# A chunked state scan on one NeuronCore: where TensorE waits for a sum, where VectorE adds it, and which engines weight and normalise

## The reference

```
states  = einsum('bcqgn,bcqgr,bcqgrp->bcgrpn', bc, to_end * dtc, xc)      # weighted x, outer product with B
h      -> h * chunk_decay + states                                         # scan over chunks
decay   = where(lower, exp(acum_i - acum_j), 0)                            # exponents of pairs of tokens
cb      = einsum('bcign,bcjgn->bcijg', cc, bc)                             # scores C.B
y_diag  = einsum('bcijg,bcijgr,bcjgr,bcjgrp->bcigrp', cb, decay, dtc, xc)
y_off   = einsum('bcign,cbgrpn,bcigr->bcigrp', cc, h_prev, exp(acum))
y       = y_forward + y_backward + d * x
y       = y * silu(z);   y = y * rsqrt(mean over the group of y*y + eps) * gain
```

## Time and profile before

| | |
|---|---|
| median of 3 runs | 3049.53 us (3045.53 to 3053.0) |
| the profiled execution, whole | 3047.3 us |
| its span, first to last instruction | 3045.6 us |
| mean granted TensorE clock, share of full | 0.983 |
| busy, share of the span | TensorE 94%, VectorE 57%, ScalarE 47%, GpSimd 16% |
| states stage | from 215.5 to 255.8 us |
| outputs stage | from 255.8 to 357.3 us |

### The profile page before, as it was taken

One profiled execution on the slowest core, in us unless ns is written; L12 is line 12 of the kernel. 1 busy time (PEld: TensorE's weight loads), 2 busy tenths in 40 slices (PEclk: granted clock), 3 DMA queues, 4 the chain that ended last, 5 costly groups with the idle time before them and its releaser, 6 DMA issues. The chain is left out here.

```text
span 3045.6 us, 37978 instructions
## 1 busy us (share of the span) xinstructions
PE 2876.4 (94%) x15242; PEld 2347.3 (77%) x15242; DVE 1738.3 (57%) x1950; ACT 1421.9 (47%) x1904; POOL 474.0 (16%) x581
## 2 busy tenths in 40 slices
PE   8998899898999899999999899999999998899998
PEld 4877797786887487777777478788888896788887
DVE  4437546445645788888888364555544316455543
ACT  4346427346223477887887132543333325443332
POOL 0002114123101623222222100000000003000000
PEclk9999899999999999999999999999999999899999
DMA  5220201112753589999999551123332301223331
GB/s 210 56 65 1 85 7 56 28 56 93 225 180 111 202 321 366 363 365 371 375 385 366 217 199 66 56 85 97 111 98 83 105 25 56 77 87 97 97 103 48
DMA packets 278527, 456.11 MB, mean 150 GB/s; under 512 B 24881, under 2 KB 206897, under 8 KB 258257
## 3 DMA queue, kind: packets, MB, share of 16 engines
q1 hardware_dynamic: 251856, 398.90, 37.2%
q0 software_dynamic: 26496, 54.79, 5.0%
HBM read 451.23 MB, written 39.08 MB: 161 GB/s over the span
## 5 line engine op out<-in xcount | busy, mean ns | idle before, releaser
L277 DVE TENSOR_TENSOR weight_part<-weights,weight_part 128x2048 fp32r<-128x2048 f32 (+1 forms) x62 | 140.5, 2267 | 153.5 <-ACT weight_part L266 153.5
L1206 ACT ACTIVATE up_conv<-banks,tap_columns 128x512 f32<-128x512 f32 x88 | 68.7, 781 | 288.4 <-PE banks L324 288.4
L266 ACT ACTIVATE weight_part<-weights 128x2048 fp32r<-128x2048 f32 (+1 forms) x62 | 115.9, 1870 | 164.1 <-PE banks L319 157.8
L1250 DVE SCALAR_TENSOR_TENSOR up_conv<-banks,tap_columns,up_conv 128x511 f32<-128x511 f32 x88 | 65.9, 749 | 214.1 <-ACT up_conv L1206 214.1
L319 PE MATMUL banks<-hT_r,weight_part 128*128 128x512 f32 x448 | 175.6, 392 | 0.3 <-PEq L3951 0.3
L324 PE MATMUL banks<-hT_r,weight_part 128*128 128x512 f32 x448 | 175.0, 391 | 0.0
L794 POOL TENSOR_SCALAR branch_mean<-branch_mean 128x1 f32<-128x1 f32 x20 | 10.7, 537 | 1047.8 <-ACT up_conv L788 704.8
L277 DVE TENSOR_TENSOR weight_part_o<-weights,weight_part_o 128x2048 fp32r<-128x2048 f32 (+2 forms) x46 | 100.0, 2174 | 115.2 <-ACT weight_part_o L266 115.2
L319 PE MATMUL banks<-hT_r,weight_part_o 128*128 128x512 f32 x384 | 149.5, 389 | 0.0
L323 PE MATMUL banks<-h_low,weight_part 128*128 128x512 f32 x384 | 149.4, 389 | 0.0
L323 PE MATMUL banks<-h_low,weight_part_o 128*128 128x512 f32 x384 | 149.4, 389 | 0.0
(11 more groups left out here) (742 smaller groups left out, 8701.0 us busy)
## 6 DMA issues: line engine op xcount, KB each, us to landing
weights<-in_w_e_gate SPq DMA_DIRECT2D x44, 1024.0 KB, 15.7
weights<-in_w_e_up SPq DMA_DIRECT2D x44, 1024.0 KB, 18.3
hT<-in_w_e_down SPq DMA_DIRECT2D x44, 1024.0 KB, 18.5
weights<-in_w_up SPq DMA_DIRECT2D x88, 512.0 KB, 4.9
gate_up<-in_w_e_gate SPq DMA_DIRECT2D x22, 1024.0 KB, 15.8
gate_up<-in_w_e_up SPq DMA_DIRECT2D x22, 1024.0 KB, 18.3
down<-in_w_e_down SPq DMA_DIRECT2D x22, 1024.0 KB, 18.6
weights<-in_w_down SPq DMA_DIRECT2D x20, 1024.0 KB, 4.9
```

The source lines that it names most:

```text
L266: c.nc.scalar.activation(self.pair(n)[0][:, 0:z], self.raw[n % RAW_SLOTS][:, 0:z], ACT.Copy).then_inc(self.high_ready, 1)
L277: c.nc.vector.tensor_tensor(low[:, 0:z], self.raw[n % RAW_SLOTS][:, 0:z], high[:, 0:z].bitcast(F32), ALU.subtract).then_inc(self.low_ready, 1)
L1206: nc.scalar.activation(a[:, f % 2, v], c.ps[:, 2 * (f % 4) + v], ACT.Identity, scale=conv[:, 2, ch:ch + 1], bias=bias[:, ch:ch + 1]).then_ ...
L1250: nc.vector.scalar_tensor_tensor(a[:, f % 2, v, 1:], c.ps[:, 2 * (f % 4) + v, 0:SEQ - 1], conv[:, 1, ch:ch + 1], a[:, f % 2, v, 1:], ALU.m ...
```

## The change

In the states, every item is weighted by two engines: GpSimd takes the first ten heads (640 columns), ScalarE the other six. TensorE waits for both. ScalarE's other work moves to earlier items, and two instructions that make `own` (the left sides of the exponent matmuls) move from the start of the outputs into the states. Twelve matmuls on the identity are added at the end of the states, behind a wait for the last but one state. `own` now lies in the space of B_T that held the SiLU and skip buffers, and these get a tensor of their own.

In the outputs, TensorE's wait for `ready` moves from ahead of the masks to behind the exponents. VectorE's sum moves ahead of the decays and the mix of the next unit. The norm moves from VectorE to GpSimd, behind the reciprocal root.

The diff, cut to its changed lines and what they stand in:

```diff
@@ -24,6 +24,7 @@
 DT_Z, ST_Z = 16, 6
+POOL_HEADS = 10
@@ -2151,6 +2152,7 @@
             masks = c.rounded(tri)
+            own = c.rounded(bT)[:, :, 0:2 * P]
@@ -2275,26 +2277,31 @@
                 act.wait_ge(wt_ready, 2)
-                for i in range(1, len(plan), 2):
+                for i in range(len(plan)):
...
                     to, rows, weights = weighs(i)
-                    for hd in range(SSD_H):
+                    for hd in range(POOL_HEADS, SSD_H):
...
                     last.then_inc(weighted[1], 1)
-                    if i == 1:
+                    if i == 0:
...
                         nc.scalar.activation(building_r, c.ps[:, 7], ACT.Copy).then_inc(rounded, 1)
-                    if i == 5:
+                    if i == 3:
...
                             nc.scalar.activation(exponents[:, :, hd], terms, ACT.Identity, scale=column(MOVES + hd), bias=column(STAYS + hd))
-                act.wait_ge(z_half, 1)
-                act.wait_ge(weighted[0], 2)
-                silu(0)
-                silu(1)
-                c.split.high(c, act)
+                    if i == 4:
+                        for d in range(2):
+                            nc.scalar.activation(own[:, :, d * P:(d + 1) * P], terms, ACT.Identity, scale=column(OWN + d), bias=column(ONE + d))
+                    if i == 6:
+                        act.wait_ge(z_half, 1)
+                        act.wait_ge(weighted[0], 4)
+                        silu(0)
+                        silu(1)
+                    if i == 7:
+                        c.split.high(c, act)
@@ -2302,12 +2309,13 @@
                 pool.wait_ge(wt_ready, 2)
-                for i in range(0, len(plan), 2):
+                for i in range(len(plan)):
...
                     to, rows, weights = weighs(i)
-                    nc.gpsimd.tensor_tensor(to.rearrange("p (h q) -> p h q", q=SSD_P), rows.rearrange("p (h q) -> p h q", q=SSD_P),
-                                            weights.unsqueeze(2).to_broadcast([P, SSD_H, SSD_P]), ALU.mult).then_inc(weighted[0], 1)
+                    n = POOL_HEADS
+                    nc.gpsimd.tensor_tensor(heads4(to[:, 0:n * SSD_P]), heads4(rows[:, 0:n * SSD_P]), weights[:, 0:n].unsqueeze(2).to_broadcast([P, n, SSD_P]),
+                                            ALU.mult).then_inc(weighted[0], 1)
@@ -2325,7 +2333,8 @@
                                 last.then_inc(z_half, 1)
-                    pe.wait_ge(weighted[i % 2], i // 2 + 1)
+                    for made in weighted:
+                        pe.wait_ge(made, i + 1)
@@ -2333,6 +2342,8 @@
                 assert len(left) <= ST_Z * (len(plan) - 1)
+                pe.wait_ge(kept, len(plan) - 1)
+                warm(c, 0, 12)
@@ -2352,7 +2363,7 @@
                         nc.vector.tensor_tensor(new, new, psum, ALU.add).then_inc(kept, 1)
-                    if i == 2:
+                    if i == 1:
@@ -2360,13 +2371,11 @@
         E = c.sb(s, "decays_of_pairs", [P, 3, 2, HG, P])
-        own = c.sb(s, "exponent_weights", [P, 2, NT, P], F32R)
+        gates = c.sb(s, "silu_and_skip", [P, 4, GP])
...
         rs = c.sb(s, "z_rstd", [P, SSD_G * NT])
-        lent = [bT[:, i, 0:CTX] for i in range(SSD_G)]
-        sz, skip = lent[0:2], lent[2:4]
+        sz, skip = [gates[:, n] for n in (0, 1)], [gates[:, n] for n in (2, 3)]
         sq = c.sb(s, "squares", [P, GP])
-        built = c.sem("so_exponents_built")
@@ -2387,7 +2396,6 @@
         def _(pool):
-            pool.wait_ge(built, 1)
@@ -2403,6 +2411,8 @@
                 nc.gpsimd.tensor_tensor(rs[:, at], rs[:, at], c.half[:, 0:1], ALU.pow).then_inc(rooted, 1)
+                pool.wait_ge(rooted, j + 1)
+                nc.gpsimd.tensor_scalar(rows_of(j), rows_of(j), rs[:, at], None, ALU.mult)
@@ -2411,20 +2421,18 @@
                     block_rows = slice(32 * g, 32 * g + 32)
-                    if i >= 2:
-                        pe.wait_ge(ready, i - 1)
-                        if lates(i - 1):
-                            pe.wait_ge(silud, lates(i - 1))
+                    if i >= 2 and lates(i - 1):
+                        pe.wait_ge(silud, lates(i - 1))
...
                                          start=True, stop=False)
-                    if i == 0:
-                        pe.wait_ge(built, 1)
                     for d in range(2):
-                        last = nc.tensor.matmul(c.ps[:, b + 1 + d], own[block_rows, d, tile], exponents[block_rows, tile].rearrange("p h n -> p (h n)"),
+                        last = nc.tensor.matmul(c.ps[:, b + 1 + d], own[block_rows, tile, d * P:(d + 1) * P], exponents[block_rows, tile].rearrange("p h n -> p (h n)"),
...
                     last.then_inc(decayed, 1)
+                    if i >= 2:
+                        pe.wait_ge(ready, i - 1)
@@ -2456,10 +2464,6 @@
 
-            for d in range(2):
-                last = nc.scalar.activation(own[:, d], terms, ACT.Identity, scale=column(OWN + d), bias=column(ONE + d))
-            last.then_inc(built, 1)
-            act.wait_ge(built, 1)
@@ -2479,10 +2483,6 @@
             L = lambda ins: c.vlink(dve, ins)
-
-            def norm(j):
-                dve.wait_ge(rooted, j + 1)
-                nc.vector.tensor_scalar(rows_of(j), rows_of(j), rs[:, j:j + 1], None, ALU.mult)
@@ -2500,16 +2500,14 @@
                     L(nc.vector.tensor_tensor(off[:, 0:GP], off[:, 0:GP], skip[j % 2], ALU.add))
+                    dve.wait_ge(diag, j + 1)
+                    nc.vector.tensor_tensor(rows_of(j), off[:, 0:GP], c.ps[:, 4 * (j % 2), GP:2 * GP], ALU.add).then_inc(ready, 1)
...
                     nc.vector.tensor_tensor(E[:, i % 3, 0], E[:, i % 3, 0], c.ps[:, 4 * (i % 2), 0:P].unsqueeze(1).to_broadcast([P, HG, P]), ALU.mult).then_inc(mixed, 1)
-                if i >= 4:
-                    norm(i - 4)
                 if i:
-                    dve.wait_ge(diag, j + 1)
-                    nc.vector.tensor_tensor(rows_of(j), off[:, 0:GP], c.ps[:, 4 * (j % 2), GP:2 * GP], ALU.add).then_inc(ready, 1)
@@ -2520,8 +2518,6 @@
                     c.split.low(c, dve)
-            for j in range(U - 3, U):
-                norm(j)
 def exponent_rows():
```

## The result

The changed kernel takes 3028.84 us in the median of six runs (3022.22 to 3033.18); the kernel before, timed beside it, 3052.17. One of the six executions of the kernel before was a slow one, 3255.83 us; the ratio leaves it out, and the median without it is 3051.34. The ratio is 0.9917, with a 95% interval from 0.9899 to 0.9935; the quotient of the two medians, 3028.84 / 3051.34 = 0.9926, lies inside it. The forecast was 3028. The execution that was profiled here took 3033.18 us with a span of 3031.5. That is 14.1 us less than the span of before, while the median won 23.3 (22.5 without that one execution).

The account below looks back on a forecast made before the run. In the outputs TensorE was taken to wait for a sum standing in VectorE's line behind another unit's exponentials. Terms -2.8 - 2.1 - 18.0 + 1.5 = -21.4 us from 3049.5 gave 3028, range 3021 to 3040.

Parts of the forecast that it names:

- The steady part: Outputs: TensorE no longer waits, so seven pairs of units take 9.68 us each, 67.8 against 85.8: -18.0 us.
- The room at the mix: Outputs: VectorE ends the mix at 5.3 us, TensorE needs it at 5.8, so 0.5 us to spare.
- The slow spells: Outputs: TensorE at granted clock 0.50 behind holes, costing 6.4 us over seven pairs; expected to go with the holes.
- The start of the outputs: First late unit's z starts 6.1 us behind the start of the outputs, not 8.21: -2.1 us (-2.5 to -1.5).
- The end of the outputs: From last SiLU to transposes, now 4.29 us: later last sum, longer last norm, +1.5 us (+0.5 to +2.5).
- The states: Shared weighting lets the outputs start at 253.0 to 253.1 against 255.79: -2.8 us (-3.2 to -1.8).
- The norm on GpSimd: Outputs: the moved norm costs GpSimd 0.85 us, hidden, coming later than the decays; hole taken as 0.
- signs of being wrong: Holes ahead of L2438, decays over 0.69 or gates over 0.43 us, norm over 1.05, or 0.50 clock without a hole.
- (a): Rival: half the holes in the outputs stay, 1 us a pair; gain -12 us, 3037; chance 0.17.
- (c): Rival: the wait for the sum becomes a wait for the mix, only the ends gain; -3.4 us, 3046; chance 0.06.
- (b): Rival: the holes go but slow spells stay, the clock falling for another cause; -15 us, 3034; chance 0.10.
- (d): Rival: GpSimd and VectorE always exclude each other, 13.1 us a pair; slower by 2.5 us, 3052; chance 0.05.

Follow-up runs that it names:

- holes_filled: The kernel before with six waste matmuls put into each hole ahead of a late unit's masks: seven pairs 79.28 us against 85.83, whole ratio 0.9995.
- states_only: The changed kernel with both order edits undone and the norm back on VectorE: transposes 3.5 us ahead of the kernel before, ratio 0.9987.
- no_warm: The changed kernel without the twelve added matmuls at the end of the states: transposes 2.4 us later than in the changed kernel, ratio 0.9924.
- norm_twice: The changed kernel with a second, unused 128x176 multiplication on GpSimd in each unit: seven pairs 66.91 us, whole 3024.89 us, run once.
- order_undone: The changed kernel with TensorE's wait and VectorE's sum both put back in their old places: 3043.96 us, ratio 0.9967.
- wait_undone: The changed kernel with only TensorE's wait for the older sum put back ahead of the masks: seven pairs 72.03 us, ratio 0.9943.
- sum_undone: The changed kernel with only VectorE's sum put back behind the mix of the next unit: seven pairs 68.52 us, ratio 0.9933.

## Why the prediction was right

The sum was -21.4 us; at the transposes it was -23.5. That is the number to hold against the sum, since both profiles start the first weighting at 216.0. The median, 3028.84 against a forecast of 3028, is closer than the working deserves. The kernel before was timed 2.6 us higher than the 3049.53 that I started from, the gain was 1.9 larger than forecast, and the two nearly cancel. The second measurement of the same kernel won 32.7 us.

The text also says that its terms span -25 to -17. Their own bounds add up to -23.2 to -16.3 (-3.2 - 2.5 - 18.0 + 0.5, and -1.8 - 1.5 - 15.5 + 2.5). The measured -23.5 lies just outside, by a term that I had not counted: the overlap of matmuls below.

- **The steady part** was put at -18.0 and was -19.2. The mechanism is shown: undone, the hole came back at 1.41 us; undone by halves, at 0.58 and 0.23. I had taken the pair at the sum of its parts, 9.68, and it took 9.48. The early unit was counted to the end of its diagonal product, 3.40 us. With no hole behind it, the masks of the next unit start at 303.07, before that product's row ends at 303.26, and the early unit takes 3.22. With 0.02 from the late unit that is 0.2 us a pair, 1.4 us in seven. The room at the mix was put at 0.5 us and was 0.44.
- **The slow spells** were put down to the holes, for 6.4 of the 18.0. `holes_filled` shows it, with 6.5, and so do the kernels with holes of 0.58 us or less, none of which has a spell in the pairs. Not every hole brings one: in the kernel before, four of the seven ahead of late units did. What decides it stays open.
- **The start of the outputs** was put at -2.1 and was 8.21 - 5.69 = -2.5. The table of exponentials was loaded while TensorE made the first exponents, so the first mix held nothing up: it was over at 257.54, and its diagonal product started at 257.93. I had allowed 0.4 us for it. `states_only` shows the same 8.85 us from the start to the first SiLU, so this term comes with the states part and not with the order. It hangs on the clock as well: in `no_warm` the first z starts 261.12 - 252.58 = 8.54 us behind the start, no sooner than the 8.21 of before, although `own` and the table are early there too. The working took a start at full clock for granted, and named the waits for `own` and the table alone.
- **The end of the outputs** was put at +1.5 and was 5.32 - 4.29 = +1.0. With the norm back on VectorE it is 4.97, so the order costs 4.97 - 4.29 = 0.68 (put at 1.0) and the norm's move 0.35 (put at 0.5).
- **The states** were put at -2.8 and were -2.7. That all shifts by 0.4 from the first weighting was about right: a weighting took ScalarE 1.54 us, and the last one started 246.40 - 246.07 = 0.33 sooner. The added matmuls set the start of the outputs, as forecast; they delay it by 0.5 us and not by 0.1. The sum gave them no worth at all, and `no_warm` shows a gain of 2.3 us, which stands in the term of the start.
- **The norm on GpSimd** was priced at 0.85 us and took 1.00. It was hidden, as forecast, but not for the reason that I gave. I had it come behind the decays. In one unit of a pair it does (304.23, beside the mix), in the other it lies over them (297.63 beside 297.93), and there it cost them 0.03 us. Two of the signs of being wrong did show: at the start the first decays took 1.10 us for 0.69 beside GpSimd's skip terms (and `low` 2.75 for 2.29), and two norms took 1.33 and 1.34. Neither reached TensorE. The Trainium skill (SBUF — State Buffer, Who interferes with whom) says that instructions of the two that both read through the shared port exclude each other. The 0.645 us of the addition in `norm_twice`, the 1.10 and the 1.33 agree in kind; the decays of 0.72 us under a norm of 0.94 do not, for by that rule they would have waited until the norm was over at 298.57, and they were over themselves at 298.65. The spans of GpSimd are rough, and no run here parts the reasons. The prediction's "to the hundredth" is also too strong: held to the end of GpSimd's instruction, a decay of 1.22 us would have ended 1.22 after it and not 1.08. For the kernel's time it did not matter, since VectorE is not the bound.
- **The rivals.** Half the holes staying (a) and a late mix (c) are out by the windows: TensorE is busy 79.4 of 80.8 us. Spells without holes (b) are out in the outputs. The two engines in series (d) did not come even with more work on GpSimd.

The forecast's 3 us of scatter is about what lies between the two medians of the changed kernel, 3028.84 and 3025.37. Its single executions lie between 3018.44 and 3033.18. What the profiles show of the cause was not in my text: the clock elsewhere in the kernel. What sets where those spells fall was not tried and stays open.

## What to carry to other kernels

A wait that ends late may wait for work whose inputs have been there for long: look what stands ahead of it in its engine's line, and move either the work up or the wait down; both moves go at the same hole, so the second is worth less once the first is made (here 1.7 or 5.2 us, where the first alone won 15.7 or 12.2). A short hole in TensorE can cost twice, once as idle time and once as the half clock behind it, and a few wasted matmuls tell the two apart. Judge an edit of a few microseconds by the stretch that it touches, from one landmark to the next, when the same stretch repeats to 0.02 us and the whole scatters by 10.

## What the runs showed of the hardware

- In `order_undone` holes of TensorE of 1.41 us, one ahead of each late unit but the first, were followed by a granted clock of 0.50 behind every second one. Holes of 0.58 and of 0.23 us never were in the outputs (`wait_undone`, `sum_undone`).
- The change from SiLU to the exponential cost ScalarE 301.75 - 300.44 = 1.31 us from the end of the one to the start of the other, 1.28 of it the table load.
- A multiplication by a value for each partition of 128x256 took GpSimd 0.94 us in the median of sixteen (0.93 to 1.34), and VectorE 0.35.
- A VectorE addition of two SBUF operands, 128x512, took 1.10 us for 0.69 beside a GpSimd multiplication of two tensors, and 0.72 under a GpSimd multiplication by one value for each partition that had started 0.30 us before it.
